# The delta rule's scan in a two-block transformer kernel: the second group of four heads starts eleven turns after the first

## The reference, cut to what matters

```python
kk = jnp.einsum('bhnid,bhnjd->bhnij', k, k)
lower = jnp.where(strict, beta[..., :, None] * kk * decay, 0.0)
sol = lax.linalg.triangular_solve(lower, rhs, left_side=True, lower=True, unit_diagonal=True)
...
def step(state, inp):
    delta = u_c - jnp.einsum('bhcd,bhde->bhce', w_c, state)
    o = jnp.einsum('bhcd,bhde->bhce', q_c, state) + jnp.einsum('bhij,bhje->bhie', a_c, delta)
    state = ge[..., None, None] * state + jnp.einsum('bhcd,bhce->bhde', k_c, delta)
```

## Time and profile before

| what | value |
|---|---|
| median of the runs | 2769.91 us |
| profiled execution | 2772.57 us |
| its span, first to last instruction | 2771.2 us |
| PE busy | 2631.6 us (95%) |
| DVE busy | 1393.1 us (50%) |
| ACT busy | 909.4 us (33%) |
| POOL busy | 160.8 us (6%) |
| mean granted PE clock | 0.978 of full speed |
| the scan with z beside it | about 212 to 415.5 us of the span |

### The profile page before, as it was taken

The page is one execution under the profiler, slowest core; times in us unless marked ns, Lnnn a source line. Parts: engine busy times, 40 slices in busy tenths (PEclk is TensorE's granted clock), DMA queues, the critical chain, the costliest instruction groups (busy, mean ns, idle before and its releaser), DMA issues.

```text
span 2771.2 us, 34182 instructions
## 1 busy us (share of the span) xinstructions
PE 2631.6 (95%) x14939; PEld 2207.0 (80%) x14939; DVE 1393.1 (50%) x1679; ACT 909.4 (33%) x1254; POOL 160.8 (6%) x177
## 2 busy tenths in 40 slices
PE   6998999989999999999999999899999999999998
PEld 4877888878878877787788977678888888788887
DVE  5665544254455346556455347566553454443433
ACT  4332213153334443222342247432122322322222
POOL 0002210000000010000012100010000100100001
PEclk9999999999999999999999999999999999999999
DMA  3220001311233325364221200056632222222221
GB/s 118 76 78 30 18 17 61 106 62 61 74 139 106 107 81 193 132 217 152 76 99 61 92 16 1 31 182 213 212 107 91 92 91 97 86 94 104 91 101 67
DMA packets 39302, 265.74 MB, mean 96 GB/s; under 512 B 4256, under 2 KB 4640, under 8 KB 8944
## 3 DMA queue, kind: packets, MB, share of 16 engines
q1 hardware_dynamic: 29520, 205.67, 21.4%
q0 software_dynamic: 8256, 55.41, 5.7%
q10 hardware_dynamic: 1376, 2.47, 0.2%
HBM read 261.43 MB, written 2.10 MB: 95 GB/s over the span
## 4 chain that ended last, share of the span: by engine, by line
PE 81%; DVE 11%; ACT 6%; issue 2%; DMA 0%; DVEq 0%; ACTq 0%
PE bank L142 79%; ACT w_hi L148 2%; DVE w_lo L151 2%; DVE ada_acc L159 1%; ACT tmp L148 1%; DVE tmp L159 1%; PE bank L145 1%; DVE dd L151 1%; ACT da_p L148 1%; DVE heads_t L159 1%; ACT L148 1%; DVE da_stat L162 1%; DVE h_lo L159 0%; DVE v_t L159 0%; ACT f_hi L148 0%
## 5 line engine op out<-in xcount | busy, mean ns | idle before, releaser
L142 PE MATMUL bank<-h_hi,w_hi 128*128 128x512 f32 (+1 forms) x1992 | 802.1, 403 | 19.7 <-DVE w_lo L151 12.9
L142 PE MATMUL bank<-h_hi,w_lo 128*128 128x512 f32 (+1 forms) x1992 | 785.4, 394 | 0.0
L142 PE MATMUL bank<-h_lo,w_hi 128*128 128x512 f32 (+1 forms) x1992 | 750.7, 395 | 4.4 <-DVE h_lo L151 4.4
L151 DVE TENSOR_TENSOR w_lo<-w_raw,w_hi 128x2048 fp32r<-128x2048 f32 (+2 forms) x197 | 445.1, 2259 | 345.8 <-ACT w_hi L148 345.8
L148 ACT ACTIVATE w_hi<-w_raw 128x2048 fp32r<-128x2048 f32 (+2 forms) x197 | 370.6, 1881 | 311.7 <-PE bank L142 301.8
L142 PEld LDWEIGHTS bank<-h_hi,w_hi 128*128 128x128 f32 (+1 forms) x1992 | 379.5, 191 | 103.9 <-DVE w_lo L151 16.2
L142 PEld LDWEIGHTS bank<-h_lo,w_hi 128*128 128x128 f32 (+1 forms) x1992 | 378.3, 190 | 91.5 <-DVE h_lo L151 10.9
L142 PEld LDWEIGHTS bank<-h_hi,w_lo 128*128 128x128 f32 (+1 forms) x1992 | 379.2, 190 | 75.7 <-issue 1.0
L142 PE MATMUL bank<-f_hi,w_hi 128*128 128x512 f32 x672 | 263.6, 392 | 1.1 <-DVE w_lo L151 1.1
L142 PE MATMUL bank<-f_hi,w_lo 128*128 128x512 f32 x672 | 262.6, 391 | 0.0
L142 PE MATMUL bank<-f_lo,w_hi 128*128 128x512 f32 x672 | 249.3, 391 | 0.0
(11 more groups left out here) (332 smaller groups left out, 3264.8 us busy)
## 6 DMA issues: line engine op xcount, KB each, us to landing
w_raw<-in_pack_ffn SPq DMA_DIRECT2D x60, 1024.0 KB, 4.9
ada_w<-in_ada_w POOLq DMA_DIRECT2D x48, 1024.0 KB, 5.3
w_raw<-in_pack_mlp SPq DMA_DIRECT2D x32, 1024.0 KB, 5.1
w_raw<-in_pack_gdn_qkv SPq DMA_DIRECT2D x12, 1024.0 KB, 4.9
w_raw<-in_pack_sc_cu SPq DMA_DIRECT2D x8, 1024.0 KB, 4.9
w_raw<-in_pack_ffn SPq DMA_DIRECT2D x8, 768.0 KB, 4.3
w_raw<-in_pack_gdn_z SPq DMA_DIRECT2D x4, 1024.0 KB, 4.9
w_raw<-in_pack_gate_a SPq DMA_DIRECT2D x4, 1024.0 KB, 5.2
```

Of the source, the lines that this page charges most:

```text
L142: return self.engine.matmul(*a, **k) if self.engine is not None else self
L151: return self.engine.tensor_tensor(*a) if self.engine is not None else self
```

## The change: the second group starts eleven turns later

On every engine the second group's generator is put behind eleven empty turns (`later`). `in_turn` and `beside` are as they were, and an empty turn counts as a turn. When the first group begins a chunk, the second is in the middle of its own, and the other way round. Both groups still do the same instructions; two memsets of `tt` move ahead of the loop.

```diff
-        qkv_made(G)
-        G.memset(t["tt"][HB:P, :, 0:HB], 0.0).then_inc(*up("pool_gdn", (grp, "tt_zero")))
-        G.wait_ge(*at("pool_gdn", (grp, "tt_zero")))
         for c in range(NCH):
...
     SCAN_PACE = (7, 2, 8)
+    SCAN_APART = 11
+
+    def later(steps, n):
+
+        for _ in range(n):
+            yield
+        yield from steps
 
     def scan_with_gate_tensor(T_, rings):
         rings.gemm, wide = rings.few, rings.gemm
-        steps = in_turn([scan_tensor(T_, rings, 0), scan_tensor(T_, rings, 1)])
+        steps = in_turn([scan_tensor(T_, rings, 0), later(scan_tensor(T_, rings, 1), SCAN_APART)])
         drain(beside(z_tensor(T_, rings, "gdn_z"), steps, *SCAN_PACE))
         drain(steps)
...
     def scan_with_gate_pool(G):
-        steps = in_turn([scan_pool(G, 0), scan_pool(G, 1)])
+        qkv_made(G)
+        for grp in range(2):
+            G.memset(scan_tiles[grp]["tt"][HB:P, :, 0:HB], 0.0).then_inc(*up("pool_gdn", (grp, "tt_zero")))
+        G.wait_ge(*at("pool_gdn", (1, "tt_zero")))
+        steps = in_turn([scan_pool(G, 0), later(scan_pool(G, 1), SCAN_APART)])
```

More of the change, by code:

```diff
@@ L1517, in scan_with_gate_scalar @@
     def scan_with_gate_scalar(S):
-        steps = in_turn([scan_scalar(S, 0), scan_scalar(S, 1)])
+        steps = in_turn([scan_scalar(S, 0), later(scan_scalar(S, 1), SCAN_APART)])
         drain(beside(z_scalar(S, "gdn_z", ("dve_scaled", ("mix", DT - 1))), steps, *SCAN_PACE))
@@ L1522, in scan_with_gate_vector @@
     def scan_with_gate_vector(V):
-        steps = in_turn([scan_vector(V, 0), scan_vector(V, 1)])
+        steps = in_turn([scan_vector(V, 0), later(scan_vector(V, 1), SCAN_APART)])
         drain(beside(z_vector(V, "gdn_z"), steps, *SCAN_PACE))
```

## The result

| kernel | median | lowest to highest | runs | profiled execution | its span |
|---|---|---|---|---|---|
| before | 2770.28 us | 2769.36 to 2770.76 | 4 | 2772.57 us | 2771.2 us |
| after | 2782.47 us | 2778.02 to 2787.17 | 4 | 2778.02 us | 2776.7 us |

The ratio after to before is 1.0043, 95% interval 1.0031 to 1.0056, so the change costs more than the 0.2% that this measurement can tell. The profiled execution of after is the fastest of its four, and that of before lies above its median. So the two traces stand only 5.5 us apart.

What follows compares the result with a forecast made beforehand. PE, busy 95% of the span, was taken as the bound, so only its scan losses counted: -17.6 - 3.0 + 3.9 + 5.7 + 10.6 + 3 = +2.6, an expected median of 2772.5 us, range 2762 to 2783 (8 in 10).

Steps and rivals of the forecast that it cites:

- the likeliest case: Whole kernel: no change that the measurement can tell, 2764.4 to 2775.4 us; chance 0.50.
- "slower" rival: Scan: DVE and ACT queues tie the groups together, 2 us at each of seven starts; +12.7, 2782.6 us; chance 0.23.
- the other 174: Scan: of its 203.5 us some 29 are lost; the other 174 are work both kernels must do.
- chunk starts two to four, and small gaps: Scan: paired waits and half clock at three starts go, 17.6 us, with 3.0 of small gaps between levels.
- starts' steady coupling: Seven one-group starts: the other group's `p` and `out` come late behind DVE; 3.9 us added, bounds 0 and 14.
- first start: First chunk: only one group's work for eleven turns, so no gain; 8.6 us lost as before, bounds 6 to 11.
- two later splits of z's weights: Scan: `w_hi` on ACT and `w_lo` on DVE now delay PE's work; together 5.7 us added, bounds 1 and 9.
- end of the scan, with its clock: Behind z's last step: one group's chain alone adds 10.6 us, bounds 8 to 12.5; half clock 3, bounds 0 and 9.
- The other split: The split of z's weights ahead of `from_state`: makes `change` and so `out` 1.2 us later.
- The sentence on the Trainium skill's rule: End of the scan: by long unbroken gaps alone it keeps full clock, 3 us less; the forecast did not follow that.

Runs made afterwards that it cites:

- e3: After with z's lead cut from 8 to 4 steps, so z reaches the end of the scan: 2777.01 us, ratio 1.0019 to before.
- e4: Before with the same cut of z's lead from 8 to 4 steps: 2775.78 us, ratio 1.0021 to before.
- 8: After with z paced at 15 turns for 4 steps, stretching z over 180 turns: 2789.04 us, ratio 1.0070 to before.
- 10: After with the second group 4 turns behind instead of 11: 2774.36 us, ratio 1.0012 to before.
- e9: After with the second group 1 turn behind instead of 11: 2764.41 us, ratio 0.9978 to before.
- e7: After with the second group 2 turns behind instead of 11: 2762.49 us over nine runs, ratio 0.9975 to before.

## Why the prediction was wrong where it was

The time lies inside the forecast range of 2762 to 2783 but at its upper edge, and the likeliest case, no measurable change, did not come. That it lies inside is luck: the range reached so high for the sake of the "slower" rival, whose mechanism did not come, and what brought the time there was in no case of the forecast. The step that failed is one sentence of the first part: "the other 174 are work that both kernels have to do". The matmuls are the same, but not the time they take. Of the losses counted by the forecast's own steps:

| step | forecast | measured |
|---|---|---|
| chunk starts two to four, and small gaps | -20.6 | -20.6, gone |
| starts' steady coupling | +3.9 | +4.9 |
| first start | 0 | +2.3 |
| two later splits of z's weights | +5.7 | +6.2 (the last alone) |
| end of the scan, with its clock | +13.6 | +12.5 |
| **sum of these** | **+2.6** | **+5.3** |
| 52 more changes of tile shape | not in it | +7.6 to 8.8 (52 x 0.146 to 0.17) |
| scan, by the traces | | +11.9 |

- **Chunk starts: right.** The pairs of waits (1.63 or 1.21 us, then 2.27) and the fall of the clock behind them are gone at all three. (The parts of the forecast's 17.6, added up from its own rows, give 17.3.) The "slower" rival, that the queues tie the groups together at 2 us a start, is wrong: the time is the one that it named, 2782.6, but by another mechanism.
- **First start: 2.3 too low.** I took 0.4 us for the second `dd` step, which takes 0.83 in the earlier trace rows, and `low` began 0.48 us behind `change` where I had 0.1. The transpose waited 5.60, forecast 4.9. And the clock was low for longer: about 217 to 227 us, before 223 to 230.
- **Splits: right in place and order for the last one.** Its waits came to 4.6, forecast 4.9, and 1.6 of half clock was not in the forecast. The other split was to cost 1.2; only a wait of 0.41 us for `change` stands behind it, so 6.2 lies near 5.7 partly because two errors cancel. Experiments 3, 4, 8 and 10 show that what a split costs is a matter of luck in where z's steps fall, worth 3 to 6.5 us each.
- **The end: right**, in its waits and in the clock: 8.2 us of waits behind the last z step (7.0 of them behind `from_state`), 1.6 for ten run-outs of 0.16, and 2.7 for the half clock, forecast 3. The clock fell just before 418 us though no wait there was over 1.55 us. The sentence on the Trainium skill's rule (TensorE: Matmul & The Clock Gate, section HAM oscillation) had it that the clock is lost to long unbroken gaps. This end speaks against that as the whole rule, as the forecast did.
- **Shape changes: missed.** The timeline that the earlier trace rows are cut from had the price in it, had I compared the same product with different followers (`dd,pp` takes 0.47 us from 240.82 us, ahead of a 64x64 product, and 0.56 from 245.82, ahead of a z step), and the forecast itself took 0.9 us for a z step among 64x64 products and 0.8 between 128-wide ones. The Trainium skill has it as well: TensorEngine Tiling (Array Packing), section Tiling Modes, says that a change of the tiling mode drains the engine, without a figure. The runs agree that a change costs time, though none shows the drain itself, and give the figure, 0.17 us in a block by itself and 0.15 in the scan.

The sum of the measured steps is 12.9 to 14.1, 1.0 to 2.2 above the 11.9 of the traces. Part of the changes probably lies in the steps' own work terms, such as the run-outs and the first start's 14.6 us of work, so the two counts would overlap there. What stays open: why this kernel's other runs are up to 9 us slower than the traced one, the fastest. Their spans are 2.3, 6.5 and 9.1 us longer, and their mean granted clocks are 0.979, 0.976 and 0.977 beside 0.980. A thousandth of the clock is 2.8 us over the span, so the clock is the likely cause, but where it fell in them is not known.

## What to carry to other kernels

Before two streams of work are interleaved more finely, count how often the tensor engine then changes between tile shapes, and price that by the same product with different followers: it is shown as busy, never as a wait. To take two chains out of each other's way a lag of one or two turns was enough here (2764 and 2762 us, before 2770); half a chunk gave little more at the starts and cost changes, a bare end and a bare beginning (2782 us). And where long instructions are fixed to another stream's steps, such as the splits of weights here, each new pace or lag moves them, so read where they fall before reading anything else.

## What the runs showed of the hardware

- A change between 64x64 and 128-wide tiles costs 0.17 us on PE at full clock, over the two directions (58 changes, 9.9 us), and the profile shows it as busy time, not as a wait. Over ten kernels of this case the slope is 0.15 us for a change.
- The clock fell behind a pair of waits (1.63 and 2.27 us with one short transpose between the earlier trace rows) but not behind one wait of 2.86 us at 298.53 us in e4, one of 2.07 at 279.76 in e9, or one of 1.61 in e7. It fell in after's end behind many waits of 0.5 to 1.55 us. In e3, which has the same chain at the end with z's products between, it did not. The longest wait alone did not tell whether the clock fell.
